# Bias split on VectorE, state decay on ScalarE, one guard for the overflow blocks, and the pairs' gather with the rows as the stationary operand

## What is computed

```python
    def expert_block(args):
        xblk, e = args
        gt = jnp.minimum(xblk @ w_gate[e] + b_gate[e], SWIGLU_LIMIT)
        up = jnp.clip(xblk @ w_up[e] + b_up[e], -SWIGLU_LIMIT, SWIGLU_LIMIT)
        hid = (up + 1.0) * (gt * jax.nn.sigmoid(SWIGLU_ALPHA * gt))
        return hid @ w_down[e] + b_down[e]
    # each token's row goes to its 4 experts, and the results come back
    # weighted by the softmax of the 4 selected logits
```

## Time and profile before

| | |
|---|---|
| median of three runs | 1316.7 us (1315.98 to 1318.29) |
| profiled execution: time, span | 1314.01 us, 1312.2 us |
| TensorE busy with matmuls | 1235.9 us, 94% of the span |
| VectorE, ScalarE, GpSimd busy | 413.9, 190.9, 65.3 us |
| moved by DMA | 434.93 MB, 428 to 430 GB/s in most of the experts' stretch |
| chain that ended last | TensorE 82%, VectorE 8%, DMA 4%, issue 3% |
| expert products L1351 | 3264 MATMUL, 672 us |
| gathers L1270 | 192 MATMUL, 86.7 us |
| scatters L1379 | 192 MATMUL, 93.7 us |

### The profile page before, as it was taken

The page is one execution under the profiler, slowest core; times in us unless marked ns, Lnnn a source line. Parts: engine busy times, 40 slices in busy tenths (PEclk is TensorE's granted clock), DMA queues, the critical chain, the costliest instruction groups (busy, mean ns, idle before and its releaser), DMA issues.

```text
span 1312.2 us, 14478 instructions
## 1 busy us (share of the span) xinstructions
PE 1235.9 (94%) x5537; PEld 542.9 (41%) x5537; DVE 413.9 (32%) x723; ACT 190.9 (15%) x315; POOL 65.3 (5%) x115
## 2 busy tenths in 40 slices
PE   6967998999999999999999959999999999999996
PEld 5644798464333333333333313333333333332342
DVE  2876567545312213031221202130303213030233
ACT  3145310130101100110100000010001001000134
POOL 4520320100000000000000000000000000000000
PEclk8978979989999999999999979999999999999998
DMA  8912300375899999999999999899999999999801
GB/s 308 324 48 71 126 11 1 112 256 240 370 430 430 427 430 428 428 429 429 429 430 427 430 388 392 372 427 429 430 428 429 428 429 429 428 427 428 343 0 40
DMA packets 46485, 434.93 MB, mean 331 GB/s; under 512 B 6264, under 2 KB 11781, under 8 KB 21857
## 3 DMA queue, kind: packets, MB, share of 16 engines
q1 hardware_dynamic: 41641, 431.54, 79.2%
q10 hardware_dynamic: 4800, 2.80, 0.8%
HBM read 430.32 MB, written 4.11 MB: 331 GB/s over the span
## 4 chain that ended last, share of the span: by engine, by line
PE 82%; DVE 8%; DMA 4%; issue 3%; ACT 2%; POOL 1%; SPq 0%; DVEq 0%; ACTq 0%; PEldq 0%; POOLq 0%
PE ps L1351 48%; PE ps L1379 7%; PE ps L1270 7%; PE ps L964 4%; PE ps L1082 4%; DMA ring<-in_w_up 3%; DVE h_region L1567 3%; PE ps L1181 2%; PE ps L1165 2%; PE ps L1340 2%; PE ps L1017 1%; DVE x_resid L1593 1%; PE ps L1172 1%; PE ps L1097 1%; PE ps L1293 1%
## 5 line engine op out<-in xcount | busy, mean ns | idle before, releaser
L1351 PE MATMUL ps<-ring,ht_region 128*64 128x512 f32 (+1 forms) x2176 | 448.8, 595 | 1.3 <-DMA ring<-in_w_up 1.3
L1351 PEld LDWEIGHTS ps<-ring,ht_region 128*64 128x64 f32 (+1 forms) x2176 | 144.7, 134 | 291.1 <-issue 291.0
L1351 PE MATMUL ps<-ring,q_region 128*64 128x512 f32 (+1 forms) x1088 | 223.2, 594 | 0.0
L1934 DVE TENSOR_SCALAR q_region<-ps 128x1024 f32<-128x1024 f32 x16 | 19.6, 1225 | 377.0 <-PE ps L1351 376.9
L1351 PEld LDWEIGHTS ps<-ring,q_region 128*64 128x64 f32 (+1 forms) x1088 | 71.7, 134 | 144.2 <-issue 144.2
L1017 PE MATMUL ps<-ht_region,ring 128*128 128x320 f32 x320 | 96.0, 461 | 0.3 <-PE ps L1017 0.3
L1379 PE MATMUL ps<-u_region,h_region 128*128 128x512 f32 (+1 forms) x192 | 93.7, 621 | 0.0
L1270 PE MATMUL ps<-h_region,u_region 128*128 128x512 f32 x192 | 86.7, 601 | 0.0
L1922 DVE TENSOR_TENSOR x_resid<-ps,x_resid 128x512 f32<-128x512 f32 (+1 forms) x96 | 66.1, 689 | 61.6 <-PE ps L1379 59.8
L1941 DVE TENSOR_SCALAR q_region<-ps 128x1024 f32<-128x1024 f32 x16 | 19.6, 1224 | 196.6 <-PE ps L1351 196.6
L1017 PEld LDWEIGHTS ps<-ht_region,ring 128*128 128x128 f32 x320 | 65.2, 205 | 29.2 <-issue 6.9
(11 more groups left out here) (359 smaller groups left out, 864.4 us busy)
## 6 DMA issues: line engine op xcount, KB each, us to landing
ring<-in_w_gate SPq DMA_DIRECT2D x64, 2048.0 KB, 24.2
ring<-in_w_up SPq DMA_DIRECT2D x64, 2048.0 KB, 15.1
ring<-in_w_down SPq DMA_DIRECT2D x64, 2048.0 KB, 19.9
ring<-in_w_in SPq DMA_DIRECT2D x5, 2048.0 KB, 16.9
ring<-in_w_out SPq DMA_DIRECT2D x2, 2048.0 KB, 12.7
ring<-in_w_ple_gate SPq DMA_DIRECT2D x1, 4096.0 KB, 24.2
x_resid<-in_x_prompt SPq DMA_DIRECT2D x4, 512.0 KB, 3.6
out<-ring ACTq DMA_DIRECT2D x1, 2048.0 KB, 9.9
```

The source lines that it names most:

```text
L1351: ins = mm(PS[s0_:s0_ + width, b0 + hf, :], lhs[:, k, s0_:s0_ + width], w[a_][:, kk, hf * 512:(hf + 1) * 512], start=False, stop=(k == KT ...
```

## The change

- **Biases.** Three transfers on 128 partitions, issued ahead of `w_in`, instead of nine behind it. VectorE splits them (three casts, two subtractions of 768 elements) between the row transposes and the small sums; ScalarE issues twelve transfers inside the SBUF that bring the parts to their 96 rows. GpSimd no longer does any of it. `bias_split` is now VectorE's signal, `bias_ready` that of the twelve transfers.
- **State decay.** GpSimd's four operations go; ScalarE does 32 activations of 128 x 128 with the decay as scale, behind its copies of keys and values, and signals `s0_scaled`.
- **Overflow.** Each engine has one `If(n_ov > 0)` around one loop.
- **Gather.** `gather_rows_turned` does in each pair what `gather_turned` does before the loop. The copies to `xg` and the eight transposes of it go; a pair has 11 uses of the two banks. Next comes the transposition of the hidden rows, then the scatter.

```diff
-OV_FIRST = 2
...
-        bias_f = ring[0:3 * E, 6, 0:3072]
+        bias_w = ring[:, 6, 0:768].rearrange("p (m f) -> p m f", m=3)
+        bias_p = [ring[:, 6, 768 + i * 384:1152 + i * 384].bitcast(BF16).rearrange("p (m f) -> p m f", m=3) for i in range(3)]
...
+            for m, n in enumerate(("b_gate", "b_up", "b_down")):
+                sp.dma_start(bias_w[:, m, :], d[n][0].rearrange("e (q f) -> (e q) f", q=4)).then_inc(bias_in, 16)
             for i, b in enumerate(IN_ORDER):
                 sp.dma_start(ring[:, i, :].rearrange("p (k c) -> p k c", k=KT),
...
-            for m, n in enumerate(("b_gate", "b_up", "b_down")):
-                for part in range(3):
-                    sp.dma_start(bias_f[part * E:(part + 1) * E, m * FF:(m + 1) * FF], d[n][0]).then_inc(bias_in, 16)
...
-            with sp.Fori(0, OV_FIRST) as j:
-                with sp.If(j < n_ov):
-                    overflow_block(j)
-            with sp.If(n_ov > OV_FIRST):
-                with sp.Fori(OV_FIRST, OV_MAX) as j:
+            with sp.If(n_ov > 0):
+                with sp.Fori(0, OV_MAX) as j:
                     with sp.If(j < n_ov):
                         overflow_block(j)
...
-            second, third = slice(E, 2 * E), slice(2 * E, 3 * E)
-            pool.wait_ge(bias_in, 16 * 9)
-            step(g.tensor_copy(bias3, bias_f))
-            step(g.tensor_tensor(bias3[second], bias_f[second], bias3[second], ALU.subtract))
-            step(g.tensor_tensor(bias_f[third], bias_f[third], bias3[third], ALU.subtract))
-            step(g.tensor_copy(bias3[third], bias_f[third]))
-            step(g.tensor_tensor(bias3[third], bias_f[third], bias3[third], ALU.subtract), bias_split)
...
-            pool.wait_ge(s0_in, 16)
-            is_drained(pool, "egs")
-            is_filled(pool, "kqs")
-            for h in range(HEADS):
-                step(g.tensor_tensor(s0[:, :, h, :], s0[:, :, h, :],
-                                     egs[:, h, :].unsqueeze(2).broadcast_to([P, DB, P]), ALU.mult), g_ready)
...
+            act.wait_ge(bias_split, 1)
+            for i in range(3):
+                for q in range(4):
+                    act.dma_start(bias3[i * E:(i + 1) * E, :].rearrange("e (m q f) -> e m q f", m=3, q=4)[:, :, q],
+                                  bias_p[i][q::4]).then_inc(bias_ready, 16)
...
+            is_filled(act, "kqs")
+            for h in range(HEADS):
+                for b in range(DB):
+                    step(a.activation(s0[:, b, h, :], s0[:, b, h, :], ACT.Copy, scale=egs[:, h, b:b + 1]),
+                         s0_scaled if b == DB - 1 else None, h + 1)
...
-                        aux(0, xg[:, 0:512], PS[:, 6 + (13 * half) % 2, :])
-                        aux(1, xg[:, 512:1024], PS[:, 6 + (13 * half + 1) % 2, :])
-                        aux(8, hidf[:, 0:512], PS[:, 6 + (13 * half + 8) % 2, :])
-                        aux(9, hidf[:, 512:1024], PS[:, 6 + (13 * half + 9) % 2, :])
+                        aux(2, hidf[:, 0:512], PS[:, 6 + (AUX * half + 2) % 2, :])
+                        aux(3, hidf[:, 512:1024], PS[:, 6 + (AUX * half + 3) % 2, :])
                         aux(10, SgT[1 - half][:, :, :],
...
+            def gather_rows_turned(k0, fills):
+
+                for hf in range(2):
+                    ps, sm_ = fills(k0 + hf)
+                    c0 = hf * RPP * P
+                    for k in range(4):
+                        for t in range(NT):
+                            last = mm(ps[:, k * P:(k + 1) * P], h3[:, t, c0 + k:c0 + RPP * P:RPP], Ssel[:, t, :],
+                                      start=(t == 0), stop=(t == NT - 1))
+                    last.then_inc(sm_, 1)
...
-                            l = 13 * half + k
+                            l = AUX * half + k
...
                         pe.wait_ge(pair_sel, pair + 2)
-                        gather(0, aux)
+                        gather_rows_turned(0, aux)
+                        pe.wait_ge(hid_act, pair + 1)
+                        turn(2, aux, ubuf)
 
                         pe.wait_ge(y_act, pair + 1)
                         pe.wait_ge(v_mark, VM["ybuf_zero"])
                         for t, (t0, n) in enumerate(TILES):
                             for hf in range(2):
-                                ps, sm_ = aux(2 + 2 * t + hf)
+                                ps, sm_ = aux(4 + 2 * t + hf)
                                 mm(ps[0:n, :], SgT[1 - half][:, t, 0:n], ybuf[:, hf * 512:(hf + 1) * 512],
                                    start=True, stop=True).then_inc(sm_, 1)
-                        pe.wait_ge(hid_act, pair + 1)
-                        turn(8, aux, ubuf)
                         ps, sm_ = aux(10)
                         for t in range(NT):
                             ins = tr(ps[:, t * P:(t + 1) * P], Sgat[:, t, :])
                         ins.then_inc(sm_, 1)
-                        turn(11, aux, xg)
...
+            dve.wait_ge(bias_in, 16 * 3)
+            for i in range(3):
+                step(v.tensor_copy(bias_p[i], bias_w), bias_split if i == 2 else None)
+                if i < 2:
+                    step(v.tensor_tensor(bias_w, bias_w, bias_p[i], ALU.subtract))
...
+                        aux(0, v.tensor_tensor, *scaled_turn(auxbank(0), 0))
+                        aux(1, v.tensor_tensor, *scaled_turn(auxbank(1), 4))
                         for t, (t0, n) in enumerate(TILES):
                             for hf in range(2):
-                                k = 2 + 2 * t + hf
+                                k = 4 + 2 * t + hf
                                 xs = x3[0:n, t, hf * 512:(hf + 1) * 512]
                                 aux(k, v.tensor_tensor, xs, auxbank(k)[0:n, :], xs, ALU.add)
-                        aux(11, v.tensor_tensor, *scaled_turn(auxbank(11), 0))
-                        aux(12, v.tensor_tensor, *scaled_turn(auxbank(12), 4))
```

More of the change, by code:

```diff
@@ L66 @@
 OV_USES = 10
+AUX = 11
 ROOT_D = D_MODEL ** -0.5
@@ L277, in trunk_kernel @@
         bias_split = sem("bias_split")
+        bias_ready = sem("bias_ready")
         wrout_in = sem("wrout_in")
         h3_zero = sem("h3_zero")
+        s0_scaled = sem("s0_scaled")
         chunk_in = [sem(f"chunk_in{c}") for c in range(TURN)]
@@ L397, in trunk_kernel @@
         for b in (6, 7):
-            fills[b] += 13 * TURNS
+            fills[b] += AUX * TURNS
         for t in range(NT):
@@ L782, in _ @@
             evacuate(16)
-            act.wait_ge(bias_split, 1)
+            act.wait_ge(bias_ready, 16 * 12)
             copy(outrow[0:PH, 3072:3584], bank("npp")[0:PH, :], "npp")
@@ L916, in overflow_block @@
                 ovaux(19, SgT[0][:, 2, :], PS[:, 7, 0:128], last=True)
-            with act.Fori(0, OV_FIRST) as j:
-                with act.If(j < n_ov):
-                    overflow_block(j)
-            with act.If(n_ov > OV_FIRST):
-                with act.Fori(OV_FIRST, OV_MAX) as j:
+            with act.If(n_ov > 0):
+                with act.Fori(0, OV_MAX) as j:
                     with act.If(j < n_ov):
@@ L1282, in _ @@
             first_banks = [fill("xta"), fill("xtb")]
-            pe.wait_ge(bias_split, 1)
+            pe.wait_ge(bias_ready, 16 * 12)
             for ps in first_banks:
@@ L1331, in aux @@
                         def aux(k):
-                            l = 13 * half + k
+                            l = AUX * half + k
                             b, m = 6 + l % 2, l // 2
-                            pe.wait_ge(drained[b], base[b] + m + i * 13)
+                            pe.wait_ge(drained[b], base[b] + m + i * AUX)
                             return PS[:, b, :], filled[b]
@@ L1359, in turn_body @@
                         pe.wait_ge(pair_sel, pair + 1)
-                        pe.wait_ge(drained[6], base[6] + i * 13 + 7 * half)
-                        pe.wait_ge(drained[7], base[7] + i * 13 + 6 * half)
+                        pe.wait_ge(drained[6], base[6] + i * AUX + 6 * half)
+                        pe.wait_ge(drained[7], base[7] + i * AUX + 5 * half)
                         if n_ov is not None and half == 0:
@@ L1406, in _ @@
             for b in (6, 7):
-                pe.wait_ge(drained[b], base[b] + 13 * MID)
+                pe.wait_ge(drained[b], base[b] + AUX * MID)
             pe.wait_ge(y_act, 2 * MID + 1)
@@ L1466, in overflow_block @@
                 turn_gates(18)
-            with pe.Fori(0, OV_FIRST) as j:
-                with pe.If(j < n_ov):
-                    overflow_block(j)
-            with pe.If(n_ov > OV_FIRST):
-                with pe.Fori(OV_FIRST, OV_MAX) as j:
+            with pe.If(n_ov > 0):
+                with pe.Fori(0, OV_MAX) as j:
                     with pe.If(j < n_ov):
@@ L1477, in _ @@
             for b in (6, 7):
-                seen[b] += 13 * TURNS
+                seen[b] += AUX * TURNS
             pe.wait_ge(tail_in, 16 * 4)
@@ L1736, in state_add @@
             def state_add(h):
```

(17 more changed lines are left out.)

8 lines of the change are left out of this document (5 added, 3 removed).

## The result

The changed kernel takes **1359.0 us** (median of 4 runs, 1357.71 to 1360.4), the kernel before, run beside it, 1317.49 (1315.98 to 1320.23): ratio 1.0313, 95% interval 1.0292 to 1.0334. It is slower by 41.5 us in the medians. The profiled execution of the changed kernel has a span of 1357.4 us against 1312.2, so 45.2 us have to be found in the traces. The forecast was 1373, the range 1348 to 1396.

What follows compares the result with a forecast made beforehand. TensorE sets the loop's pace, with DMA just as full. Gather +73, clock +8, late chunks -1.3, bias split -16 and overflow code -7 give +57 us on 1314.0, so 1371, or about 1373 as median; range 1348 to 1396.

Steps and rivals of the forecast that it cites:

- The gather: In each loop pair, strided weight loads 0.232 us apart lengthen the small work: +4.6 us a pair, +73 us in 16.
- The late chunks: In the loop, TensorE's two waits for weight chunks go because pairs outlast their DMA: -1.3 us.
- The clock: In the loop, TensorE's clock falls in strided gathers and some falls outlast them: 0.5 us a pair, +8 us.
- The bias split: Before the loop, VectorE's convolutions no longer wait for GpSimd's subtractions: -16 us, bounds -10 to -20.
- The decay: Before the loop, GpSimd's 7.83 us go and idle ScalarE gets some 11 us: no effect either way.
- The overflow code: Between the loop's halves, one jump in place of three leaves a third of the code fetching: -7 us, bounds 0 and -11.
- the clock rival: In the loop, the clock falls in every pair and outlasts the gather: +28 instead of +8, 1393 us; chance 0.17.
- the asymmetry stated first: In the loop's pairs, time saved is mostly lost again to DMA, while time added is paid sixteen times.
- the loads hide: In the loop's gather, loads hide behind matmuls, pairs shorten by about 1.6 us until DMA decides: about 1290 us; chance 0.08.

Runs made afterwards that it cites:

- contiguous gather: The changed kernel with h3 written in another column order, so that each weight load's 128 columns lie side by side: 1284.93 us, ratio 0.9766 to the kernel before.
- gather alone: The kernel before with only the new gather and its order of small work: 1382.94 us, ratio 1.0514.
- all but the gather: The changed kernel with the old gather and old order of small work, keeping the new biases, decay and overflow code: 1294.48 us, ratio 0.9847.
- 192 instructions: The kernel with the contiguous gather plus 192 instructions that do nothing ahead of all of TensorE's code, run once: span 1286.9 us.
- guard alone: The kernel before with only the single If around the overflow loop: 1309.97 us, ratio 0.9954.
- bias split alone: The kernel before with only the bias split moved from GpSimd to VectorE, its transfers changed too: 1301.02 us, ratio 0.9876.

## Why the prediction was right, point by point

**The gather: right to a tenth.** +4.6 us a pair was said, +4.56 measured; a period of 62.4 was said, 62.41 measured. Its parts: the gather 451.88 - 440.58 = 11.30 (said 11.1, with 0.232 us a load; 0.2355 measured), the eight transposes with their wait 1.61 (said 1.8; the wait is 0.31 to 0.39, said 0.5), the scatter 5.96 (5.85), `Sgat` 0.38 (0.4). The step that carried it was to read the price off the one place where the kernel before already did the same access, and not off the contiguous matmuls. The assumption that 128 rows cost what 64 do holds (0.2355 against 0.232). The rule quoted there (the Trainium skill, "TensorE: Matmul & The Clock Gate", section "LDWEIGHTS (loading the stationary operand)"), 107 ns a load, can hold for columns 4 bytes apart (0.114 us from load to load); 16 bytes apart the trace does not agree, and the measured 0.2355 decides.

**The late chunks: right.** In the changed kernel no wait for a chunk of the loop is left, and TensorE alone sets the pace.

**The clock: the one term whose mechanism failed, 8 us said, 0 measured.** Windows of TensorE over the whole first and second half of the loop, kernel after (window, length, PE busy, granted clock, DMA share, GB/s), and one inside a gather with all engines' columns as in the earlier trace rows:

```profile
287.00:785.00 498.00, 494.98 (x2150) 1.00 0.93 391
806.00:1300.00 494.00, 491.06 (x2303) 1.00 0.91 382
...
445.00:452.00 7.00, 7.00 (x33) 7.00 (x33) 0.69 (x1) 0.00 (x0) 0.00 (x0) 1.00 1.02 433
```

In the gather the array gets 128 columns in 0.2355 us, where 0.114 would do, and in both windows the clock is 1.00; only between them, behind the hole (785 to 806 us), it is 0.92. The failed step is that a fall seen in the first pair's gather was carried over to the loop's gathers. The fall itself goes with the strided loads of that first gather. TensorE in the changed kernel, and in the one with the contiguous gather, where the first gather is contiguous too, each about 4 us behind the clock's rise to full, in this order:

```profile
281.90:283.90 2.00, 2.00 (x9) 2.00 (x9) 0.00 (x0) 0.00 (x0) 0.00 (x0) 0.50 0.00 0
```

```profile
281.70:283.70 2.00, 1.28 (x9) 0.59 (x9) 1.73 (x7) 1.21 (x2) 0.00 (x0) 1.00 0.00 0
```

In all eight kernels with a strided first gather in which the clock rose to 1.00 there, it fell back to 0.50 inside that gather; in the three with a contiguous one in which it rose, it stayed. (In the gather alone, in all but the gather and with 192 instructions it did not rise there.) The contiguous gather ends by 281.7 us, so that it was also over sooner. Why the same access lowers the clock there and not in the loop, where it follows on 43 us of products, is open.

The DMA share of 0.93 and 0.91 is the 0.94 that was said. The rival built on it, +28, had been given 0.17. All products of 64 matmuls in the timeline from 287 to 490 us take 13.95 or 13.96 us; the one behind the hole takes 15.65, as it took 15.73 in the earlier trace rows.

**The bias split: right in its cause, 16 said, 13.65 measured in the trace and 15.6 in the medians of that part alone.** Timelines, kernel after: the end of the last convolution on VectorE, VectorE's part of the split, ScalarE's issues of the transfers, and the table load behind them.

```profile
67.56 0.93 DVE L1570 SCALAR_TENSOR_TENSOR h_region<-q_region,vecs,h_region 128x64 f32<-128x64 f32 x3
68.52 0.16 DVE L1586 COPY small<-ps 128x4 f32<-128x4 f32 x1
...
17.70 0.56 DVE L1546 CAST ring<-ring 128x768 bf16<-128x768 f32 x1
18.29 0.96 DVE L1548 TENSOR_TENSOR ring<-ring 128x768 f32<-128x768 f32 x1
...
26.37 0.16 DVE L1553 TENSOR_TENSOR small<-ps,small 128x4 f32<-128x4 f32 x1 [4.93 <-PE ps L996]
...
21.52 8.63 ACTq L704 DMA_DIRECT2D bias_s<-ring  x12
...
30.18 1.28 ACT L739 ACT_TABLE_LOAD   x1 [17.29 <-issue]
```

The last convolution ends at 68.5 in place of 83.72: 15.2 us, said 16 (66.6 and about 1 taken back). VectorE's part fits into the idle stretch, of which 4.93 us are left, so it costs nothing. The twelve issues take 8.63 us from 21.52 (said 4 to 9 from near 21.5) and make the table load 2.75 us late (30.18 against 27.43 in the earlier trace rows); the convolution has made this up. The other 1.6 us, between 68.5 and the loop, I did not locate. They are inside what kernels with the same code before the loop differ by: it starts at 300.46, 302.50 and 305.56 us in three (and at 300.86 with the decay moved), mean of the four 302.3. In the six with VectorE's split and the same strided first gather it starts between 283.09 and 287.11, mean 285.2: 17.1 us earlier, so the 16 that was said is no worse than the 13.65 of one pair of traces. The granted clock there differs as well: in the stretch from 27 to 33 us it was 0.84 before and 0.56 after, but 0.64 with the guard alone and 1.00 with the bias split alone, so it does not go with the change.

**The decay: right**, 0 said, +0.1 measured with an interval of 0.9988 to 1.001.

**The overflow code: right in kind, mis-sized.** -7 was said with a bound at -11, -11.8 measured, outside the bound. The term started from the 13.85 us of the chain's row, but the hole is 15.30, from 763.40 to 778.70. Of it 3.52 stay, more than the 2.89 of VectorE that the bound left: the bound's own reasoning gives -12.4 from 15.30. And less than the third of the hole that the forecast reckoned with stays, 3.52 of 15.30. The guard alone is worth -5.6 in the trace, close to the -7; what was not foreseen is that guard and gather act together. That the hole is the fetching of code stays unproven.

**The sum.** 57 was said on the profiled execution, 45.2 came: -8 for the clock, -4.8 for the hole, +2.4 for the bias split, -1.0 left over in the halves, and a remainder below 1. The two largest errors had the same sign, which left the result 14 us below the forecast (the offset of 2.7 us between profiled execution and median is in that too) and inside the range. (The upper end of that range, 1396, is said to be where the clock rival ends, which was priced at 1393; the result touches neither.) Of the asymmetry stated first both sides were seen: a pair 4.56 us longer is paid 16 times (+67.1 for the gather alone), and the contiguous gather, whose small work is 13.40 us (425.01 to 438.41) against 14.53, gives all of it back in waits. The 28.8 us by which its span is below that of the kernel before lie outside the pairs: 17.5 before the loop (it starts at 282.93; 3.9 of this it has over the changed kernel, whose first gather is strided and lasts 4.1 us longer) and 11.8 in the hole. This kernel is also the test of the rival *the loads hide*, which was priced at about 1290.

## What to carry to other kernels

Before a layout is given to TensorE's stationary side to save transposes, look for one place in the trace where an operand with that spacing is already loaded, and take the distance of the loads from there; here a load of 0.2355 us that feeds only 128 columns (0.114 us) had nothing to hide behind. If the spacing is the price, write the producer's output in another order: the column order of `h3` was free, one ScalarE access pattern, and turned +3.1% into -2.3%. Where two engines both seem full, ask for each edit in which direction it moves: time added is paid in full, time saved stops at the other engine. And where GpSimd and VectorE work side by side, equal lengths in both timelines of instructions that are otherwise short are a sign to move the work, which here was worth 15.6 us.

## What the runs showed of the hardware that was not expected

- Loading an fp32 stationary operand of 128 columns takes 0.114, 0.121, 0.177, 0.2355 and 0.241 us at 4, 8, 12, 16 and 32 bytes from column to column: 1.84 ns for each 16-byte piece touched, up to one piece a column, fits them within 3% from 8 bytes on.
- A TensorE that is kept by strided loads at half its columns for 11.5 of 62.4 us kept its granted clock at 1.00 in both halves of the loop but for the first product behind the hole (15.65 us in place of 13.95), though in the first pair's gather, with the same spacing, it fell to 0.50 each time that it had risen; and in the contiguous kernel the clock was at 0.59 and 0.57 for 4 us behind two of ten waits of up to 2.18 us for a chunk, and not behind the others.
- TensorE stood for 15.0 to 15.9 us where it passes the overflow code that isn't run, 11.5 with the new gather, 9.5 to 9.7 with the guard and 3.5 with both. An instruction packet of 16 KB starts 5.5 to 7 us behind the start of the hole in all of them, also where TensorE has gone on by then. What decides is open; shifts of the code by 64 to 192 instructions did not change the 3.5.
